# Two filter sums moved into the first product, and a wider first tile behind the switch to normed tokens, in a 16-product forward pass

## The chip, the cores and the metric

One NeuronCore of one Trainium2 chip runs the whole program in one launch. The metric is the device time of that launch in microseconds (us); a lower one is better. Matrices are float32; the weights and tokens of the large products are split into a high and a low part (type fp32r), and each 128x128 weight block is used in three matmuls: high by high, high by low, low by high.

## The reference, cut to what matters

Two blocks of a transformer run one after the other on 256 tokens of width 1024. What the change touches is the Conformer convolution at the very start and the gated feed-forward products of the second block.

```python
def conformer_conv(h, w_pw1, b_pw1, w_dw, b_dw, ln_g, ln_b, w_pw2, b_pw2):
    u = h @ w_pw1 + b_pw1                      # "pw1": 16 tiles of 128 channels
    a, gate = jnp.split(u, 2, axis=-1)
    u = a * jax.nn.sigmoid(gate)
    u = causal_depthwise_conv(u, w_dw) + b_dw  # width 31: the filter sums
    u = jax.nn.silu(layernorm(u, ln_g, ln_b))
    return u @ w_pw2 + b_pw2                   # "pw2": 8 tiles

def _swiglu(h, wg, wu, wd):                    # "gu2", "gu3": gate and up, 44 tiles
    return (jax.nn.silu(h @ wg) * (h @ wu)) @ wd
...
h = _rms_norm(x, norm_ffn[l]) * (1.0 + sc2) + sh2
x = x + g2 * _swiglu(h, ffn_gate[l], ffn_up[l], ffn_down[l])
```

## The kernel before

Sixteen products run in a fixed order on TensorE (PE): pw1, pw2, gu0, dn0, mixd, outd, gu1, dn1, mixe, oute, gu2, dn2, mixo, outo, gu3, dn3. Channels lie on partitions, the 256 tokens on the free axis. A product has tiles of 128 output channels; a tile takes `kts` blocks (8 in most products), a block is three matmuls, so a tile of 8 blocks has 24 matmuls. All PE matmuls of the products have one line, L558. The first tiles of a product (its `lead`, 4 in pw1 and 3 in gu2) run interleaved block by block; the others run one after the other. PSUM banks go round: five in pw1, six in gu2 and gu3.

Weights come in units of eight blocks (512 KB). The SP queue loads unit v into one of five `raw` buffers once VectorE (DVE) has made the low part of unit v-5. ScalarE (ACT) makes the high part (`whi`), DVE the low part (`wlo`), both about five units ahead of PE. Each engine has its own instruction queue, worked in order, and the order is written out by hand in four programs that loop over the same tiles.

The convolution stage. In pw1 the even tiles are gates and the odd ones values. DVE takes each tile from its bank (`tmp<-ps`), ACT applies the sigmoid on even tiles, and DVE writes the gated tile `U[n]` after each odd one. The causal filter needs shifted copies of U, and gets them through memory: `taps_out(j)` writes U of channel tile j to the tensor `uscr` (one DMA of 143.5 KB on ACT's queue, for tile 7 on SP's), and `taps_in(j)` reads it back shifted into `UR[j % 3]` with four DMAs of 142 KB. For j = 0, 1, 2 ACT issues these reads, at the pw1 tiles that `READ_BACK` names (9, 11, 13); for j = 3 to 7 SP issues them, after it has waited for the last U and written it to `uscr`. On PE, `taps(j)` (line L598) is the filter sum of channel tile j: 64 matmuls of 32 columns of diagonal filter blocks `DG[j % 3]` by `UR[j % 3]`, into bank 5 or 6. It waits for `DG`, for all four reads of `UR` and, from j = 2, for the copy of an earlier sum out of its bank. All eight filter sums stand behind pw1. At pw1 tile 7 SP also writes an attention table to memory (`scratch<-bvec`, 432 KB from 12 partitions).

```python
READ_BACK = (9, 11, 13)
...
product("pw1", ..., after, ...)      # calls after(nt) when tile nt is issued
for j in range(KD):
    taps(j)
```

The feed-forward stages of the second block. gu2 and gu3 (f = 2, 3) start before the norm of their tokens is known: tiles 0 to 5 use raw tokens and 258 columns, 256 tokens and two that carry a shift. Meanwhile ACT and DVE prepare normed tokens in the other pair of buffers (`HH`, `HL`), the low part in `normed_low(kt)`, which signals `nhl`; from tile 6 on (`NORMED`) PE uses these and 256 columns, waiting for `nhl` block by block. `broad(nt, kt)` says which blocks of a feed-forward product move 258 columns although 256 would do: in gu0 and gu1 all of tile 3 (`BROAD_TILE`), in dn0 to dn3 the first four blocks of the leading tiles, in gu2 and gu3 none behind tile 5. In the products of `BROAD_AFTER`, pw1 among them, the first three blocks after other matmuls are also made wide (`fresh`). The two extra columns lie behind the tokens at T:T+2; DVE fills them once at the start and signals `edge`.

Of the kernel before, what the change touches and what calls it, by code (L numbers as in the profile page):

```python
# [14 lines left out]
T = 256  # L15
D = 1024
KD = 8
# [37 lines left out]
SHIFT = 4  # L55
GATHERED = 6
RINGED = 3
READ_BACK = (9, 11, 13)


class Product:
# [156 lines left out]
NORMED = {2: 6, 3: 6}  # L218
NORMED_PUT = {2: "oute", 3: "outo"}
# [177 lines left out]
def program(nc, wall, ada, x_in, vec_in, crow_in, wq_in, row_in, rel_in, k128, kdist, koh, kmask, kbias, scratch, uscr, out):  # L397
    with ExitStack() as ctx:
        S = Signals(lambda name: ctx.enter_context(nc.semaphore("s_" + name)))
# [13 lines left out]
        HH = [sb(f"HH{i}", [P, KD, TW], F32R) for i in range(2)]  # L413
        HL = [sb(f"HL{i}", [P, KD, TW], F32R) for i in range(2)]
        RST = [sb(f"RST{i}", [P, T]) for i in range(2)]
        SQA, SQB = sb("SQA", [P, T]), sb("SQB", [P, T])
        ident, ones, bones = sb("ident", [P, P]), sb("ones", [P, P]), sb("bones", [P, P])
# [71 lines left out]
        def end_mm(name):  # L489
            return PROD[name].tile_mm[slot_of(name, PROD[name].tiles - 1 - (PROD[name].tiles - 2 in PROD[name].double))]  # L490
# [25 lines left out]
        def tensor_program():  # L516
            pe = Queue(nc.tensor)
# [70 lines left out]
            def convolution():  # L588
                def taps(j):

                    bk = bank[5 + j % 2]
                    pe.wait_ge(S.dg, j + 1)
                    pe.wait_ge(S.ur[j % 3], 64 * (j // 3 + 1))
                    if j >= 2:
                        pe.wait_ge(S.cva if j - 2 < SHIFT else S.lnx, j - 1)
                    for m in range(8):
                        for r in range(4):
                            ins = pe.e.matmul(bk[32 * r:32 * r + 32, 0:T], DG[j % 3][:, 8 * r + m, :],  # L598
                                              UR[j % 3][:, r, 4 * m:4 * m + T], start=(m == 0), stop=(m == 7))
                    pe.then_inc(ins, S.cvt)  # L600

                def over_channels(bk, t, j):

                    return pe.e.matmul(bk[:, 0:T], ones[:, :], t, start=(j == SHIFT - 1), stop=(j == KD - 1))

                def after(nt):
                    if nt == 4:
                        pe.wait_ge(S.koh, 16)
                        pe.wait_ge(S.rel, 16)
                        pe.wait_ge(S.sd, 1)  # L610
                        pe.then_inc(pe.e.matmul(bank[7][0:12, 0:NB], rels[:, :], ohs[:, :], start=True, stop=True), S.relm)

                product("pw1", HH[NORM_SET[0]], HL[NORM_SET[0]], T, norm_ready(0), after,
                        lambda kt: total(0) if kt == KD - 1 else None)
                for j in range(KD):
                    taps(j)
                    if j == SHIFT:
                        pe.wait_ge(S.bv, 1)
                        pe.wait_ge(S.lnp, SHIFT - 1)
                        pe.then_inc(pe.e.matmul(bank[7][:, 0:T], ones[:, :], SQA[:, :], start=True, stop=True), S.lnt)  # L620

                pe.wait_ge(S.cva, SHIFT + 1)
                pe.wait_ge(S.lnp, SHIFT - 1 + 2 * (GATHERED - 1))
                over_channels(bank[7], SQA[:, :], SHIFT - 1)
                pe.wait_ge(S.ev, PROD["pw1"].first_slot + PROD["pw1"].slots)
                over_channels(bank[0], SQ8[:, 0, :], SHIFT - 1)
                for j in range(GATHERED, KD):
                    pe.wait_ge(S.lnx, j + 1)
                    shift = over_channels(bank[7], CV[:, j, :], j)
                    if j == KD - 1:  # L630
                        pe.then_inc(shift, S.lnt)
                    pe.wait_ge(S.lnq, j + 1)
                    square = over_channels(bank[0], SQ8[:, j, :], j)
                pe.then_inc(square, S.lnt)
                busy(bank[5], 17)
                product("pw2", HH[LN_SET], HL[LN_SET], T, lambda kt: pe.wait_ge(S.lnl, kt + 1))

            def feed_forward(f):
                i = FFN_NORM[f]

                def after(nt):
                    if nt == 0 and f not in NORMED:
                        total(i)

                def before(kt):
                    if kt == TOTAL_AT and f in NORMED:
                        total(i)

                other = 1 - NORM_SET[i]
                later = (NORMED[f], HH[other], HL[other], T, lambda kt: pe.wait_ge(S.nhl, normed_tiles(f, kt))) if f in NORMED else None  # L650
                def broad(nt, kt):
                    return f < 2 and nt == BROAD_TILE

                def gated(kt):
                    return pe.wait_ge(S.gl, KF * f + min(kt + (2 if kt < BROAD_KTS else 1), KF))

                product(f"gu{f}", HH[NORM_SET[i]], HL[NORM_SET[i]], T + 2 if f >= 2 else T, norm_ready(i), after, before, None, later, broad)
                product(f"dn{f}", GH, GL, T, gated,
                        broad=lambda nt, kt: nt < PROD["dn0"].lead and kt < BROAD_KTS)
# [638 lines left out]
        def vector_program():  # L1298
# [187 lines left out]
            def feed_forward(f, scale):  # L1486
# [7 lines left out]
                def normed_low(kt):  # L1494
# [2 lines left out]
                    stt(HL[other][:, kt, 0:T], TX[kt % 4][:, :], mod(f - 2, 3, kt), HH[other][:, kt, 0:T].bitcast(F32),  # L1497
                        ALU.add, ALU.subtract, S.nhl)

                for s in range(2 * KF + 3):  # L1500
                    if s == 0 and f in NORMED:
                        lows(first_unit(name) + LOOK - 1)
                        inverse(NORM_RST[i])
                        normed_scaled(0)
                        normed_scaled(1)
                    if s < 2 * KF:
                        lows(low_to(name, s))
                    if s == 0 and f not in NORMED:
                        inverse(NORM_RST[i])
                    if f in NORMED and 1 <= s <= KD // 2:  # L1510
                        for kt in (2 * s, 2 * s + 1):
                            if kt < KD:
                                normed_scaled(kt)
                        normed_low(2 * s - 2)
                        normed_low(2 * s - 1)
                    if s % 2 == 0 and s >= 4:
                        m = s // 2 - 2
                        N = KF * f + m
                        dv.wait_ge(S.gh, N + 1)
                        tt(GL[:, m, :], TG[N % 3][:, :], GH[:, m, :].bitcast(F32), ALU.subtract, S.gl)  # L1520
                    if s % 2 == 0 and 2 <= s <= 2 * KF and not normed(f, s - 2):
                        N = KF * f + s // 2 - 1
                        g, u = TG[N % 3], TU[N % 2]
                        dv.wait_ge(S.silu, N + 1)
                        dv.wait_ge(S.ev, slot_of(name, s - 1) + 1)
                        if f >= 2:
                            stt(g[:, :], u[:, :], bcol[2 + N % 2][:, 0:1], g[:, :], ALU.add, ALU.mult, S.gm)
                        else:
                            tt(g[:, :], u[:, :], g[:, :], ALU.mult, S.gm)
                    if s < 2 * KF and normed(f, s):  # L1530
                        if s % 2:

                            N = KF * f + s // 2
                            g, ps = TG[N % 3], ended(name, s)
                            dv.wait_ge(S.silu, N + 1)
                            dv.then_inc(dv.e.tensor_tensor(g[:, :], ps[:, 0:T], g[:, :], ALU.mult), S.ev, 2)  # L1536
                    elif s < 2 * KF:
                        N = KF * f + s // 2
                        ps = ended(name, s)
                        if s % 2 == 0:  # L1540
                            t, b = TG[N % 3], bcol[N % 2]
                            dv.wait_ge(S.gl, max(N - 2, 0))
                            if f >= 2:
                                dv.wait_ge(S.silu, N - 1)
                        else:
                            t, b = TU[N % 2], bcol[2 + N % 2]
                            if N:
                                dv.wait_ge(S.gm, plain_pairs(f, s // 2 - 2) if s >= 4 else plain_pairs(f - 1, KF - 1) if f else 0)
                        if f >= 2:
                            dv.e.tensor_tensor(t[:, :], ps[:, 0:T], rooted(name)[:, :], ALU.mult)  # L1550
                            dv.then_inc(dv.e.tensor_copy(b[:, :], ps[:, T:T + 1]), S.ev)
                        else:
                            tt(t[:, :], ps[:, 0:T], rooted(name)[:, :], ALU.mult, S.ev)
# [625 lines left out]
```

## Time and profile before

| | us |
|---|---|
| median of three runs | 1199.04 (1198.98 to 1201.17) |
| the profiled execution, its own time | 1208.44 |
| its span | 1207.1 |
| PE busy | 1155.9 (96%) |
| VectorE busy | 883.2 (73%) |
| ScalarE busy | 655.7 (54%) |
| GpSimd busy | 84.7 (7%) |
| DMA, mean over the span | 214 GB/s |

The profiled execution took 9.4 us longer than the median of the runs. PE's busy time counts a matmul from its start to its modelled end, and matmuls overlap, so that share says only that PE has nearly always one in hand; how fast they follow each other must be read from counts in a stretch or from start times.

### The profile page before, as it was taken

How to read it: one execution, taken by the hardware profiler on the slowest of the kernel's cores; microseconds unless marked ns; L12 is line 12 of the kernel's file. 1: busy time of each engine (PE TensorE's matmuls, PEld its weight loads, DVE VectorE, ACT ScalarE, POOL GpSimd, SP SyncE). 2: the span in 40 equal slices, each digit the busy share in tenths (PEclk: the TensorE clock that was granted, in tenths of full speed). 3: DMA queues.
4: the chain of work that ended last, by engine and by line, in shares of the span. 5: the costliest groups of instructions: out<-in, count | busy, mean ns of one | idle time of the engine just before them, and what ended most of it. 6: DMA issues, size and time to landing. Idle time of an engine off the chain costs nothing.

```text
span 1207.1 us, 24464 instructions
## 1 busy us (share of the span) xinstructions
PE 1155.9 (96%) x9868; PEld 1108.5 (92%) x9868; DVE 883.2 (73%) x1645; ACT 655.7 (54%) x1153; POOL 84.7 (7%) x95
## 2 busy tenths in 40 slices
PE   7889999999998999999998889999999889999999
PEld 7859999999987999999988779999999768999999
DVE  6737698878665798887888668888886666855542
ACT  6427665445445654546555777544455776644431
POOL 2021000001000100002100011000010222000000
PEclk9999999999989999999998999999999999999999
DMA  7862698889742488887743324899987433566562
GB/s 271 252 179 105 222 323 289 265 275 316 239 158 88 140 298 287 278 292 268 273 130 111 105 88 158 269 327 321 325 277 231 142 117 122 195 192 190 176 192 71
DMA packets 81412, 258.28 MB, mean 214 GB/s; under 512 B 9032, under 2 KB 22036, under 8 KB 81300
## 3 DMA queue, kind: packets, MB, share of 16 engines
q1 hardware_dynamic: 78564, 253.94, 63.6%
q10 hardware_dynamic: 2736, 2.77, 0.8%
q8 instruction: 79, 1.29, 0.4%
q14 instruction: 33, 0.27, 0.1%
HBM read 254.01 MB, written 2.67 MB: 213 GB/s over the span
## 4 chain that ended last, share of the span: by engine, by line
PE 82%; DVE 7%; ACT 3%; issue 3%; DMA 2%; POOL 1%; ACTq 0%; DVEq 0%; POOLq 0%
PE ps L558 75%; PE ps L598 2%; DMA UR<-uscr 1%; DVE wlo L1303 1%; PE ps L663 1%; PE ps L671 1%; PE ps L662 1%; DMA raw<-wall 1%; PE ps L667 1%; ACT oS L889 1%; ACT tmp L889 1%; ACT whi L889 1%; PE ps L739 0%; ACT eS L889 0%; DVE RST L1346 0%
## 5 line engine op out<-in xcount | busy, mean ns | idle before, releaser
L558 PE MATMUL ps<-HH,whi 128*128 128x256 f32 (+1 forms) x2152 | 613.5, 285 | 12.2 <-DVE wlo L1303 7.7
L558 PE MATMUL ps<-HL,whi 128*128 128x256 f32 (+1 forms) x2152 | 603.9, 281 | 0.0
L558 PE MATMUL ps<-HH,wlo 128*128 128x256 f32 (+1 forms) x2152 | 603.9, 281 | 0.0
L889 ACT ACTIVATE whi<-raw 128x1024 fp32r<-128x1024 f32 (+1 forms) x364 | 381.0, 1053 | 313.3 <-PE ps L558 293.4
L1303 DVE TENSOR_TENSOR wlo<-raw,whi 128x1024 fp32r<-128x1024 f32 (+1 forms) x364 | 442.9, 1224 | 45.2 <-ACT whi L889 45.0
L558 PEld LDWEIGHTS ps<-HH,whi 128*128 128x128 f32 x2152 | 408.5, 190 | 23.6 <-issue 17.5
L558 PEld LDWEIGHTS ps<-HL,whi 128*128 128x128 f32 x2152 | 410.0, 191 | 0.4
L558 PEld LDWEIGHTS ps<-HH,wlo 128*128 128x128 f32 x2152 | 410.0, 191 | 0.0
L558 PE MATMUL ps<-GH,whi 128*128 128x256 f32 (+1 forms) x704 | 195.0, 277 | 1.7 <-DVE tmp L1536 1.3
L558 PE MATMUL ps<-GL,whi 128*128 128x256 f32 (+1 forms) x704 | 194.7, 277 | 0.0
L558 PE MATMUL ps<-GH,wlo 128*128 128x256 f32 (+1 forms) x704 | 194.7, 277 | 0.0
L558 PEld LDWEIGHTS ps<-GH,whi 128*128 128x128 f32 x704 | 132.3, 188 | 2.4 <-issue 1.7
L558 PEld LDWEIGHTS ps<-GL,whi 128*128 128x128 f32 x704 | 132.3, 188 | 0.0
L558 PEld LDWEIGHTS ps<-GH,wlo 128*128 128x128 f32 x704 | 132.3, 188 | 0.0
L1317 DVE CUSTOM_DVE_ANT_0 araw<-araw,cond 128x1024 f32<-128x1024 f32 x96 | 120.7, 1257 | 5.1 <-DMA araw<-ada 5.1
L1853 POOL TENSOR_TENSOR SQA<-SQA,ts 128x256 f32<-128x256 f32 x48 | 40.4, 842 | 684.8 <-ACT ts L889 684.2
L1536 DVE TENSOR_TENSOR tmp<-ps,tmp 128x256 f32<-128x256 f32 x38 | 16.1, 424 | 62.7 <-PE ps L558 60.8
L1303 DVE TENSOR_TENSOR tmp<-ps,RST 128x256 f32<-128x256 f32 x104 | 43.5, 420 | 21.4 <-PE ps L558 20.8
L889 ACT ACTIVATE GH<-tmp 128x256 fp32r<-128x256 f32 x88 | 35.6, 405 | 33.1 <-DVE tmp L1303 21.7
L1303 DVE TENSOR_TENSOR GL<-tmp,GH 128x256 fp32r<-128x256 f32 x88 | 36.9, 419 | 1.3 <-ACT GH L889 1.3
L1309 DVE SCALAR_TENSOR_TENSOR X<-ps,MOD,X 128x256 f32<-128x256 f32 x32 | 15.2, 479 | 30.4 <-PE ps L558 30.4
L598 PE MATMUL ps<-UR,DG 128*32 128x256 f32 x512 | 30.1, 396 | 7.3 <-DMA UR<-uscr 6.1
(223 smaller groups left out, 926.9 us busy)
## 6 DMA issues: line engine op xcount, KB each, us to landing
raw<-wall SPq DMA_DIRECT2D x363, 512.0 KB, 4.4
araw<-ada SPq DMA_DIRECT2D x96, 512.0 KB, 4.9
oBB<-kbias SPq DMA_DIRECT2D x16, 192.0 KB, 2.5
UR<-uscr SPq DMA_DIRECT2D x20, 142.0 KB, 3.0
UR<-uscr ACTq DMA_DIRECT2D x12, 142.0 KB, 12.0
aTB<-scratch SPq DMA_DIRECT2D x12, 128.0 KB
out<-X SPq DMA_DIRECT2D x8, 128.0 KB, 3.0
uscr<-U ACTq DMA_DIRECT2D x7, 143.5 KB, 10.1
```

What stands on the lines that cost most here:

```text
L558: ins = pe.e.matmul(o, l, r, start=(kt == p.order[0] and i == 0), stop=(kt == p.order[-1] and i == 2))
L598: ins = pe.e.matmul(bk[32 * r:32 * r + 32, 0:T], DG[j % 3][:, 8 * r + m, :], UR[j % 3][:, r, 4 * m:4 * m + T], start=(m == 0), stop=(m == 7))
L662: pe.e.matmul(bk[:, 0:128], q[:, 0:128], k[:, 0:128], start=True, stop=True)
L663: return pe.e.matmul(bk[:, 128:384], q[:, 128:256], k[:, 0:256], start=True, stop=True)
L667: ins = pe.e.transpose(bk[:, i * P:(i + 1) * P], s[:, i * P:(i + 1) * P], ident[:, :])
L671: pe.e.matmul(o, v(0), pt[:, 0:256], start=True, stop=False)
L889: ac.then_inc(ac.e.activation(o, i, func, **kw), sem)
L1303: dv.then_inc(dv.e.tensor_tensor(o, a, b, op), sem)
L1309: dv.then_inc(dv.e.scalar_tensor_tensor(out=o, in0=a, scalar=s, in1=b, op0=op, op1=op2), sem)
L1317: dv.then_inc(dv.e.tensor_tensor_reduce(a[:, :], a[:, :], cond[:, :], 1.0, 0.0, ALU.mult, ALU.add, MOD[:, v:v + 1]), S.ada)
L1536: dv.then_inc(dv.e.tensor_tensor(g[:, :], ps[:, 0:T], g[:, :], ALU.mult), S.ev, 2)
L1853: po.then_inc(po.e.tensor_tensor(o, a, b, op), sem)
```

## The change

The filter sums of channel tiles 0 and 1 are issued from within pw1, after its tiles 9 and 12; the loop behind pw1 starts at 2. ACT issues the reads of `UR` for channel tiles 0, 1 and 2 at pw1 tiles 5, 8 and 11. In gu2 and gu3 the eight blocks of tile 6, the first on normed tokens, move 258 columns. For that DVE writes the two columns behind the tokens of `HL[0]` and `HH[0]` anew at the start of gu2, and signals `edge` a second time, for which PE waits at tile 6.

```diff
-READ_BACK = (9, 11, 13)
+READ_BACK = (5, 8, 11)
+AMID = (9, 12)
...
                 def after(nt):
+                    if nt in AMID:
+                        taps(AMID.index(nt))
                     if nt == 4:
...
-                for j in range(KD):
+                for j in range(len(AMID), KD):
                     taps(j)
...
                 def broad(nt, kt):
+                    if f in NORMED and nt == NORMED[f]:
+                        pe.wait_ge(S.edge, 2)
+                        return True
                     return f < 2 and nt == BROAD_TILE
...
+                if f == 2:
+                    both = ident[:, 0:2 * KD].rearrange("p (k t) -> p k t", t=2)
+                    dv.wait_ge(S.xf, KD)
+                    dv.wait_ge(S.mm, end_mm(NORMED_PUT[f]))
+                    for t in (HL[0], HH[0]):
+                        ins = dv.e.tensor_copy(t[:, :, T:T + 2], both)
+                    dv.then_inc(ins, S.edge)
                 for s in range(2 * KF + 3):
```

## Rows read from the trace of the kernel before

**Rows 1.** The page's chain of work that ended last, shares of the span.
```profile
PE ps L558 75%; PE ps L598 2%; DMA UR<-uscr 1%; DVE wlo L1303 1%; PE ps L663 1%; PE ps L671 1%; PE ps L662 1%; DMA raw<-wall 1%; PE ps L667 1%; ACT oS L889 1%; ACT tmp L889 1%; ACT whi L889 1%; PE ps L739 0%; ACT eS L889 0%; DVE RST L1346 0%
```
**Rows 2.** L558 in stretches of gu1, gu2, gu3, outd; busy (matmuls), clock, DMA share.
```profile
425.00:515.00 90.00, 90.00 (x796) 90.00 (x795) 1.00 0.87 291
760.00:850.00 90.00, 90.00 (x766) 90.00 (x766) 1.00 0.91 315
1045.00:1135.00 90.00, 90.00 (x767) 90.00 (x766) 1.00 0.62 197
400.00:407.00 7.00, 7.00 (x62) 7.00 (x61) 1.00 0.45 154
```
**Rows 3.** PE's order of time at gu2's tiles 3 and 6, gu1's 3, outd's 2.
```profile
744.22 0.28 PE L558 MATMUL ps<-HH,whi 128*128 128x258 f32 x1
...
752.91 0.28 PE L558 MATMUL ps<-HH,whi 128*128 128x256 f32 x1
...
420.12 0.28 PE L558 MATMUL ps<-HH,wlo 128*128 128x258 f32 x1
...
396.24 0.28 PE L558 MATMUL ps<-HH,wlo 128*128 128x258 f32 x1
```
**Rows 4.** PE's order of time in gu3's tile 6, its last two blocks.
```profile
1038.00 0.38 PE L558 MATMUL ps<-HH,whi 128*128 128x256 f32 x1
...
1038.46 0.33 PE L558 MATMUL ps<-HH,whi 128*128 128x256 f32 x1
```
**Rows 5.** DVE's order of time around the normed tokens of gu3, gu2, and at the start.
```profile
1037.47 0.87 DVE L1309 SCALAR_TENSOR_TENSOR HL<-tmp,MOD,HH 128x256 fp32r<-128x256 f32 x2
...
740.57 1.75 DVE L1346 RECIPROCAL RST<-RST 128x256 f32<-128x256 f32 x1 [1.25 <-ACT RST L889]
...
17.20 0.79 DVE L1420 CAST HL<-ident 128x16 fp32r<-128x16 f32 x2
```
**Rows 6.** PE's order of time in pw1 (tiles 10, 13 begin) and at the first filter sum.
```profile
39.26 0.28 PE L558 MATMUL ps<-HH,whi 128*128 128x256 f32 x1
...
47.42 0.28 PE L558 MATMUL ps<-HH,whi 128*128 128x256 f32 x1
...
59.89 0.42 PE L598 MATMUL ps<-UR,DG 128*32 128x256 f32 x4 [4.15 <-DMA UR<-uscr]
```
**Rows 7.** ACT's order of time: weights, taps_out(3), first taps_in, copies of filter sums 2, 3.
```profile
33.23 2.00 ACT L889 ACTIVATE whi<-raw 128x1024 fp32r<-128x1024 f32 x2
...
39.98 0.33 ACTq L892 DMA_DIRECT2D uscr<-U  x1
...
41.54 3.09 ACTq L892 DMA_DIRECT2D UR<-uscr  x1
...
75.82 0.47 ACT L889 ACTIVATE CV<-ps,vec 128x256 f32<-128x256 f32 x1 [4.45 <-PE ps L598]
79.27 0.47 ACT L889 ACTIVATE CV<-ps,vec 128x256 f32<-128x256 f32 x1 [2.98 <-PE ps L598]
```
**Rows 8.** SP's scratch and last uscr, DVE's taking of pw1 tile 15.
```profile
37.95 0.90 SPq L1922 DMA_DIRECT2D scratch<-bvec  x1
...
62.72 0.33 SPq L1922 DMA_DIRECT2D uscr<-U  x1
...
61.68 0.42 DVE L1303 TENSOR_TENSOR tmp<-ps,RST 128x256 f32<-128x256 f32 x1
```
**Rows 9.** ACT's DMA queue (packets, MB, share), 41.5 to 47, 47 to 60; landing, 75 to 78.
```profile
q10 hardware_dynamic: 87, 0.09, 4.6%
...
q10 hardware_dynamic: 1036, 1.06, 29.5%
...
UR<-uscr SPq DMA_DIRECT2D x4, 142.0 KB, 2.9
```
**Rows 10.** All engines in two stretches of the first filter sum, clock last but two.
```profile
58.00:62.00 4.00, 2.11 (x24) 1.43 (x28) 1.46 (x2) 2.30 (x3) 0.00 (x0) 0.78 1.03 348
62.00:66.00 4.00, 3.24 (x44) 1.87 (x36) 1.29 (x3) 0.68 (x2) 0.00 (x0) 0.79 1.08 279
```

## The prediction

> **What bounds the kernel now.** I began with the page's chain of waits [rows 1]: PE's product matmuls carry 75% of it, and the filter sums (L598) and the reads behind them come next, at 2% and 1%. So two questions matter: how fast do product matmuls follow each other, and how long does PE stand in the convolution stage.
>
> For the first I counted L558 in stretches of one product each [rows 2]. In gu1, 90 us hold 796 matmuls, one in 113.1 ns. In gu2 and gu3 the same 90 us hold 766 and 767, one in 117.5 ns, although these move 256 columns too and no wait lies between them. So 256 columns have two paces. outd's last tiles show the slow one too (62 in 7 us). Tiles that move 258 columns have a third: from the start of gu2's tile 3 to that of tile 6 are 72 matmuls in 8.69 us, 120.7 ns each [rows 3]. What sets the pace? At gu1's last wide matmul, 420.12, PE goes over to 256 columns and the fast pace follows. Of the 20 places where the trace goes from wide to narrow, 18 lead to 113 ns at once; the two in outd, one of them at 396.24 [rows 3], to the slow pace, which then stays. gu2 and gu3 also enter tile 6 fast. Then blocks 6 and 7 wait for the normed tokens: the matmuls at 1038.00 and 1038.46 last 0.38 and 0.33 us where 0.28 is usual [rows 4], and DVE's low parts of these blocks were written just then, 1037.47 to 1038.34 [rows 5]. Behind these two small waits the pace is slow, up to the end of the product. I read: a small wait amid narrow matmuls can drop PE into the slow pace, a run of wide ones nearly always frees it.
>
> For the second I followed PE, ACT, SP and the DMA queues from 33 to 80 us. pw1 goes at 2.72 us a tile ((47.42 - 39.26) / 3) and ends at 59.89 - 4.15 = 55.74 [rows 6]. PE then waits 4.15 us for the reads of the first filter sum. They were issued from 41.54 on, the first issue alone taking 3.09 us [rows 7], and landed at about 59.9. Why so late: SP's scratch write went out at 37.95 [rows 8], and from 41.5 to 47 ACT's queue got 4.6% of the DMA engines' time, for 87 packets; from 47 to 60 ACT's queue moved 1036 packets [rows 9], and one channel tile's reads are 512. Once freed, a filter sum takes 3.45 us (79.27 - 75.82) [rows 7].
>
> **The change part by part.** *The wide first tile.* Tile 6 costs 24 x 120.7 ns = 2.90 us. Before, it took about 24 x 113.1 = 2.71 plus waits of 0.10 and 0.05 [rows 4] and the slow end of the tile, 2.9 as well: no difference. The wide tile reaches blocks 6 and 7 later by 18 x 7.6 ns = 0.14 us, so most of the small waits goes away, and what is left (I reckon some 0.03 us at block 7) falls among wide matmuls. Then 37 tiles, 888 matmuls, go at 113.1 in place of 117.5 ns: 3.9 us in gu2 and 3.9 in gu3, 7.8 together. Bounds: 0 for a product that stays slow, 3.9 for one that goes fast. The cover holds: DVE is busy 73% of the span, and DMA, at 0.91 [rows 2], would need 0.91 x 117.5 / 113.1 = 0.95; gu1 runs fast at 0.87, so a loss of up to 1 us in gu2 is possible and I take none. DVE's two copies at the start of gu2 are of the kind that took 0.79 us for two at most [rows 5]. They stand ahead of three low parts that PE needs only units later, and ahead of the reciprocal, before which DVE idles 1.25 us [rows 5]. So they cost nothing; without that cover, 0.2 to 0.8 us of later normed tokens.
>
> PE's wait for the copies is met long before tile 6. The Trainium skill ("TensorE: Matmul & The Clock Gate", Back-to-back issue gap) has a matmul cost its columns over 2.4 GHz plus 2.5 ns, that is 109 ns for 256 columns and 110 for 258. By it two columns more can't make what follows faster; the trace disagrees, as 113.1 and 117.5 ns stand for the same 256 columns. By the rule this part would cost 0.04 us and gain nothing.
>
> *The filter sums amid pw1.* First UR[0]. ACT reaches tile 5 after the two weight copies from 33.23, of which the first belongs to it, so the four reads go out from 34.2 to 36.0. That is ahead of the scratch write. The uncrowded latency is 2.9 us [rows 9], but weights and the write of U[2] share the queues; I take a landing at 41 (bounds 39 and, if the last reads get stuck behind the scratch write, 47.5). pw1's tile 9 ends at 39.26, where tile 10 now begins [rows 6], so PE waits 1.7 us, sums 3.45 us, and ends tiles 10 to 12 at 41 + 3.45 + 3 x 2.72 = 52.6.
>
> Then it needs UR[1]. ACT can issue these reads only behind the write of U[3] at 39.98 [rows 7], so from 40.35: that is the slot that UR[0] had, 1.2 us sooner, right behind the scratch write and among the same weight loads. The wait is thus not taken away, it is handed to the next channel tile. What would let UR[1] land sooner than UR[0] did at 59.9? Its reads may skip the 3.09 us stall of the issue; but before, all of UR[0] was issued by 47, and from then on its packets only took turns with SP's, so an earlier issue helps little. What would let it land later? UR[0]'s own 512 packets now stand ahead of the scratch write: at the mean rate of ACT's queue behind it, 1036 packets in 13 us [rows 9], and with the idle share of the queues before 38, I reckon 0.4 us net. I take 60.3. Bounds: 45, the uncrowded latency from 42.2 on, and 64.
>
> PE so waits 60.3 - 52.6 = 7.7 us. A wait of 4.15 us was followed by a clock of 0.78 and 0.79 over 8 us [rows 10]: half speed, 1.2 GHz, for 0.22 x 4 + 0.21 x 4 = 1.7 us of loss. I take the same 1.7 (up to 3.4 for the longer wait). pw1 ends at 60.3 + 3.45 + 1.7 + 3 x 2.72 = 73.6, where it was 55.74.
>
> Next is UR[3], which SP reads only after the last U. From DVE's taking of tile 15 to SP's write of U[7] it took 62.72 - 61.68 = 1.04 us [rows 8]; with 0.16 for the last matmul's end ahead of it and 0.35 for the write's issue, the first read goes out at 75.2, the last some 1.7 later, and 2.9 us on it has landed [rows 9]: 79.8. DG[3], queued on DVE behind the last U, is done sooner, and filter sum 2 (73.6 to 77.1) is hidden. Filter sum 3 starts at 79.8; before, it started at 79.27 - 3.7 = 75.6 [rows 7]. From there on, UR[4] to UR[7] (reads that follow each other on a queue that is then nearly empty), the sums, the layer norm and pw2 keep their old distances. So this part costs 79.8 - 75.6 = 4.2 us, plus 0.1 for the two times three blocks that go wide after the sums: 4.3.
>
> Queued behind ACT's earlier reads are its weight copies and sigmoids: UR[0]'s issue (1.8 us) delays one weight copy that DVE wants only at 37.8, UR[1]'s delays the sigmoid of tile 8 to about 44, and U[4] with it; PE, late itself, needs that bank five tiles on. SP's queue keeps its order. The weights of pw1 are five units ahead, so a unit that lands 1 to 2 us later stops nobody.
>
> The Trainium skill ("DMA: Bandwidth & Descriptors", Issuing engines are not separate DMA queues) says that transfers started by different engines run on the same 16 DMA engines and interleave. The trace agrees: ACT's queue moves 87 packets in 5.5 us while SP's holds the scratch write [rows 9]. This speaks against the change, since reads issued sooner still share.
>
> **The sum.** -7.8 + 4.3 = -3.5 us. The profiled execution, span 1207.1 and own time 1208.44, becomes 1203.6 and 1204.9. It lies 9.4 us above the median of the runs; I keep that distance: 1199.0 - 3.5 = 1195.5 us.
>
> **The rivals.**
>
> UR[1] lands in time. For it: its issue is 1.2 us earlier and may miss the stall; the scratch write comes from 12 partitions and may not hold every DMA engine. Against it: PE's wait before ended with the slowest share, and 47 to 60 was crowded throughout. Then pw1 ends at 52.6 + 3.45 + 3 x 2.72 = 64.2, UR[3] lands at 64.2 + 6.2 = 70.4, and the part gains 5.2 us (7.2 if UR[0] is in time too): 1199.0 - 7.8 - 5.2 = 1186.0, or 1184.0. The point from which part one changes sign is a landing of UR[1] at 60.3 - 4.3 = 56.0.
>
> The slow pace stays (slower). A place in gu2 and gu3, the end of tile 6: the rest of a small wait at block 7 leaves only three wide matmuls behind it, and outd went over to narrow ones slowly after nine. Price: the 7.8 us don't come, and the stage costs its 4.3: 1203.3. It decides for slower as soon as both products keep 117.5 ns and UR[1] lands after 58.5. For it: two in 20 switches. Against it: 18 in 20, and both products end tiles 3, 4 and 5 in the same rhythm, from which tile 6 was entered fast. If only one of them stays slow, the sum is -3.9 + 4.3, 1199.4, no change. By the Trainium skill's rule above, this rival is the rule: wide matmuls give nothing.
>
> UR[1] is later still, at 63 to 64, or the clock takes 3.4 us in place of 1.7: another 3 us, 1198.5, about no change. For it: UR[0]'s packets ahead of the scratch write, a wait nearly twice as long. Against it: DMA before 38 has room, and part of UR[0] fits in.
>
> **How the numbers follow.** About 0.2%, 2.4 us, is what a measurement here can tell from no change. Forecast, 0.48: 1195.5, its own range 1193.5 to 1197.5, of which I hold the part above 1196.6 for 0.08. UR[1] in time, 0.20. One product stays slow, 0.12. Both, 0.08. UR[1] or the clock later still, 0.12. By these, faster is 0.48 - 0.08 + 0.20 = 0.60, no change 0.08 + 0.12 + 0.12 = 0.32, slower 0.08. But cases can meet: one product at 117.5 ns with a late UR[1] gives 1199.4 + 3 = 1202.4, slower. For that I move 0.02 and 0.08 over: 0.58, 0.24, 0.18. The range takes in half of the rival below and of those above: 1185.5 to 1200.5.
>
> **What would show it.** In gu2 and gu3, 796 matmuls in 90 us, where 766 stood. In pw1, a filter sum from 41 to 44.5, a wait of PE at the second one of 7 to 8 us put down to UR, a clock below 1 there, the product's end near 73.6, and the copy of filter sum 3 near 83.5 where it was 79.27. The prediction is wrong if PE finds UR[1] landed (then 1186), if the first sum waits behind the scratch write, or if tile 7 of gu2 or gu3 goes at 117.5 ns.

## The result, and the profile after

The changed kernel takes 1209.0 us (median of 7 runs, 1204.71 to 1215.21), the one before 1199.04 (7 runs, 1196.89 to 1201.17). The ratio is 1.0063, with a 95% interval of 1.0041 to 1.0086: some 7.5 us slower, where 3.5 us faster was forecast. (The two medians lie 10.0 us apart, 0.83%, inside that interval; I go by the ratio.) The profiled execution of the changed kernel spans 1207.7 us; the profiled one of before spans 1207.1. In the traces the two look equal, in the timed runs they are not. That gap is the first thing to explain.

The page's chain that ended last, shares of the span, answers to [rows 1]:
```profile
PE ps L559 73%; PE ps L599 2%; DVE wlo L1309 1%; DMA UR<-uscr 1%; PE ps L669 1%; PE ps L668 1%; PE ps L677 1%; PE ps L673 1%; ACT whi L895 1%; ACT oS L895 1%; ACT tmp L895 1%; ACTq L898 1%; DVE X L1315 0%; ACT HH L895 0%; ACT eS L895 0%
```
A new link is in it, ACTq L898: ACT's issuing of the reads of UR now stands on the path.

The product matmuls (L559 after the change) in 90 us of gu2 and of gu3, as in [rows 2]; the columns are those shown there:
```profile
770.00:860.00 90.00, 90.00 (x796) 90.00 (x795) 1.00 0.94 331
1050.00:1140.00 90.00, 90.00 (x796) 90.00 (x796) 1.00 0.66 205
```
Here are the 796 matmuls that the prediction named, and gu2 and gu3 take 123.2 and 123.1 us from their start to dn2's and dn3's, where they took 127.1 and 127.1. So 7.85 us are gained between these two traces.

DVE's order of time at gu2's start, with the two copies (L1511) and the reciprocal of [rows 5]:
```profile
746.38 0.17 DVE L1511 CAST HL<-ident 128x16 fp32r<-128x16 f32 x1
746.46 0.17 DVE L1511 CAST HH<-ident 128x16 fp32r<-128x16 f32 x1
...
748.86 1.75 DVE L1352 RECIPROCAL RST<-RST 128x256 f32<-128x256 f32 x1 [1.11 <-ACT RST L895]
```
The copies take 0.17 us each, and DVE still idles 1.11 us ahead of the reciprocal: they cost nothing.

PE's order of time in pw1 and the convolution, the filter sums alone. First the kernel before (L598), of which [rows 6] shows only the start:
```profile
59.89 5.35 PE L598 MATMUL ps<-UR,DG 128*32 128x256 f32 x64 [4.15 <-DMA UR<-uscr]
67.18 3.66 PE L598 MATMUL ps<-UR,DG 128*32 128x256 f32 x64 [1.94 <-DMA UR<-uscr]
72.10 10.57 PE L598 MATMUL ps<-UR,DG 128*32 128x256 f32 x192 [1.26 <-issue]
```
Then the changed kernel (L599):
```profile
42.77 3.66 PE L599 MATMUL ps<-UR,DG 128*32 128x256 f32 x64 [2.65 <-DMA UR<-uscr]
...
58.88 6.59 PE L599 MATMUL ps<-UR,DG 128*32 128x256 f32 x64 [4.01 <-DMA UR<-uscr]
...
73.84 3.66 PE L599 MATMUL ps<-UR,DG 128*32 128x256 f32 x64
81.71 4.65 PE L599 MATMUL ps<-UR,DG 128*32 128x256 f32 x49 [4.21 <-issue]
```
The chain that ended last, around filter sum 1 (start, length, what):
```profile
41.05 4.28 ACTq L898
...
47.76 10.98 DMA UR<-uscr
58.74 0.14 issue
58.88 6.59 PE ps L599 x64
```
Before, PE waited 4.15 us for UR[0], 1.94 for UR[1] and 1.26 for UR[2], 7.4 us in all; now it waits 2.65 us for UR[0], 4.01 for UR[1], and 4.21 ahead of filter sum 3, 10.9 in all. The last is put down to "issue"; DMA issues tell what it was. SP's order of time, the write of U[7] and the reads of UR[3] and later ones:
```profile
75.05 0.33 SPq L1935 DMA_DIRECT2D uscr<-U  x1
...
75.48 13.36 SPq L1935 DMA_DIRECT2D UR<-uscr  x16
```
The four reads of UR[3] are issued from 75.48 to 76.87, and the last of them lands at 81.6, just ahead of the sum.

All engines in the stretches of filter sum 1 and filter sum 3; the last but two is the granted clock, as in [rows 10]:
```profile
58.00:65.00 7.00, 6.12 (x60) 3.30 (x64) 0.00 (x0) 0.22 (x1) 0.00 (x0) 0.51 0.96 281
81.00:86.00 5.00, 4.29 (x49) 2.83 (x53) 0.00 (x0) 0.00 (x0) 0.00 (x0) 0.66 0.80 171
```
Behind each of the two longer waits PE runs at its lower level, 1.2 GHz. The clock of 0.51 over 7 us is worth 3.4 us, but 0.9 us of that stretch passed while PE still stood waiting: sum 1 took 6.59 us where 3.66 is usual, 2.9 lost. At the second it is 0.34 x 5 = 1.7 us. pw2 starts at 108.7 us, where it started at 100.9. So this stage costs 7.8 us in these two traces, and eats what gu2 and gu3 gained. The terms: 3.5 us more of waits, 2.9 us more of half clock (4.6 against the 1.7 of before), 0.4 us because tiles 10 and 13 take 2.90 us with their wide blocks where 2.72 is usual, and 0.7 us because pw1's tile 9 begins at 37.23 in the one trace and at 36.54 in the other, before any sum was moved; in the second trace of the kernel before it begins at 37.11. That makes 7.5 of the 7.8 us, and the last 0.7 isn't shown to be the change's.

### The profile page after: what moved, and what is told of

Its sections match the earlier page's. It is cut to its first block, busy times and chain, and to the rows that moved or that the text cites. A ratio compares the mean times of both kernels' runs of the same rounds, so it can differ in the third digit from the quotient of the medians.

```text
span 1207.7 us, 24466 instructions
## 1 busy us (share of the span) xinstructions
PE 1151.0 (95%) x9868; PEld 1100.7 (91%) x9868; DVE 883.1 (73%) x1647; ACT 655.7 (54%) x1153; POOL 84.2 (7%) x95
## 4 chain that ended last, share of the span: by engine, by line
PE 81%; DVE 8%; ACT 4%; issue 3%; DMA 1%; POOL 1%; ACTq 1%; DVEq 0%; POOLq 0%
PE ps L559 73%; PE ps L599 2%; DVE wlo L1309 1%; DMA UR<-uscr 1%; PE ps L669 1%; PE ps L668 1%; PE ps L677 1%; PE ps L673 1%; ACT whi L895 1%; ACT oS L895 1%; ACT tmp L895 1%; ACTq L898 1%; DVE X L1315 0%; ACT HH L895 0%; ACT eS L895 0%
## 5 line engine op out<-in xcount | busy, mean ns | idle before, releaser
L559 PE MATMUL ps<-HH,whi 128*128 128x256 f32 (+1 forms) x2152 | 611.2, 284 | 12.5 <-DVE wlo L1309 8.0
L559 PE MATMUL ps<-HL,whi 128*128 128x256 f32 (+1 forms) x2152 | 601.6, 280 | 0.0
L559 PE MATMUL ps<-HH,wlo 128*128 128x256 f32 (+1 forms) x2152 | 601.3, 279 | 0.0
L559 PEld LDWEIGHTS ps<-HH,whi 128*128 128x128 f32 x2152 | 408.7, 190 | 24.5 <-issue 18.5
L559 PEld LDWEIGHTS ps<-HL,whi 128*128 128x128 f32 x2152 | 408.7, 190 | 0.4
L559 PEld LDWEIGHTS ps<-HH,wlo 128*128 128x128 f32 x2152 | 408.5, 190 | 0.0
L559 PE MATMUL ps<-GH,whi 128*128 128x256 f32 (+1 forms) x704 | 195.3, 277 | 1.7 <-DVE tmp L1549 1.3
L559 PE MATMUL ps<-GL,whi 128*128 128x256 f32 (+1 forms) x704 | 195.0, 277 | 0.0
L559 PE MATMUL ps<-GH,wlo 128*128 128x256 f32 (+1 forms) x704 | 194.9, 277 | 0.0
L559 PEld LDWEIGHTS ps<-GH,whi 128*128 128x128 f32 x704 | 132.3, 188 | 2.4 <-issue 1.7
L559 PEld LDWEIGHTS ps<-GL,whi 128*128 128x128 f32 x704 | 132.4, 188 | 0.0
L559 PEld LDWEIGHTS ps<-GH,wlo 128*128 128x128 f32 x704 | 132.3, 188 | 0.0
L599 PE MATMUL ps<-UR,DG 128*32 128x256 f32 x512 | 33.3, 423 | 10.9 <-DMA UR<-uscr 6.7
L599 PEld LDWEIGHTS ps<-UR,DG 128*32 128x32 f32 x512 | 19.6, 121 | 23.4 <-issue 16.1
```

The costliest lines, as they stand in the source:

```text
L559: ins = pe.e.matmul(o, l, r, start=(kt == p.order[0] and i == 0), stop=(kt == p.order[-1] and i == 2))
```

## The experiments

Two questions were open. On the pace, theory A (the prediction's) says that small waits drop PE into the slow pace and wide matmuls free it; theory B, that the pace comes and goes from one execution to the next of the same program, so that the slow gu2 and gu3 of the first trace were a chance of that execution. On the convolution, theory 1 says that UR[1] is held up by what stands beside it in the queues, SP's scratch write above all, and that sums amid pw1 delay its end and so the last U. Each kernel below was timed against the kernel before on the same chip; three sets of runs were made, and before had medians of 1201.4, 1201.45 and 1203.57 us in them.

**The wide tile alone.** The diff's part in `broad` and the two copies on DVE; the order of sums and reads as before.
```
+                    if f in NORMED and nt == NORMED[f]:
+                        pe.wait_ge(S.edge, 2)
+                        return True
```


> The wide first tile of gu2 and gu3 alone, with DVE's two copies; the filter sums stay behind pw1. Theory A (the slow pace of gu2 and gu3, 117.5 ns a matmul, is in every execution of the kernel before): 7.8 us faster, ratio 0.9935. Theory B (it was in the profiled execution of the kernel before, which took 9.4 us longer than its timed ones, and those go at 113 ns without help): the same time, ratio 0.999 to 1.001; its profile shows 113 ns in both.

Measured: 1202.37 us (12 runs), ratio 1.0009 (0.9985 to 1.0032). In its trace gu2 and gu3 take 123.2 us each. No gain of this part is seen in the timed runs; the interval leaves room for 1.8 us at most, not for 7.8.

**The sums amid pw1 and the earlier reads alone.**
```
-READ_BACK = (9, 11, 13)
+READ_BACK = (5, 8, 11)
+AMID = (9, 12)
```


> The two filter sums amid pw1 and the earlier reads alone. The profile of the change has pw2 start 7.8 us later (108.72 against 100.88), so both theories expect about 7.8 us more at the start of pw2. Theory A: the total is 7.8 us slower, 1.0065. Theory B: the total is as slow as the whole change, 7 to 10 us, 1.006 to 1.008, as the wide tile gives nothing to timed executions; should its profile fall on slow gu products, they are counted at 117.5 ns.

Measured: 1208.33 us (12 runs), ratio 1.0057 (1.0031 to 1.0083). The whole loss comes from this part. In its trace pw2 starts at 104.1: PE waits 2.88 us for UR[0], 1.95 for UR[1] and 3.22 ahead of sum 3, and sums 3 and 4 take 9.96 us where 7.11 is usual. gu2 and gu3 both go slowly in it. It is of the slowest of the kernel's 12 runs (1214.44), 6.1 us above their median.

**The kernel before, as it is.**

> The kernel before, unchanged, for a second profile of it. Theory A: 766 matmuls in 90 us in gu2 and gu3 again, and an own time of the profiled execution near the timed ones. Theory B: the pace of gu2 and gu3 differs from the first profile, and the profiled time is shorter by 3.9 us for each product that goes fast. Ratio 1.000 in both.

Measured: 1202.42 us, ratio 1.0016 (0.9993 to 1.0039). The trace spans 1199.2 us, 7.9 less than the first one of the same program. Product matmuls (L558) in gu2 and gu3:
```profile
760.00:850.00 90.00, 90.00 (x797) 90.00 (x796) 1.00 0.94 329
1043.00:1133.00 90.00, 90.00 (x797) 90.00 (x796) 1.00 0.65 203
```
The kernel without the wide tile has the fast pace in both. Its two small waits in tile 6 are there (the matmul at that place follows after 223 ns in gu2, where 113 is usual). So the waits don't decide. Nor does a run of wide matmuls: pw2 opens with three wide blocks, and behind them (L558) it is fast in the first trace of the kernel before,
```profile
104.00:116.00 12.00, 12.00 (x108) 12.00 (x107) 1.00 0.57 200
```
and slow in this second one of the same program:
```profile
107.00:119.00 12.00, 12.00 (x104) 12.00 (x103) 1.00 0.63 224
```
Theory A falls here.

**The scratch write moved.** SP writes the attention's table only after the convolution's reads.
```
-                if nt == 7:
-                    sp.wait_ge(S.bv, 1)
-                    load(scratch, bvec[:, :].unsqueeze(1).broadcast_to([12, NR, NB]), S.bd)
+                pass
...
+            sp.wait_ge(S.bv, 1)
+            load(scratch, bvec[:, :].unsqueeze(1).broadcast_to([12, NR, NB]), S.bd)
             for nt in tiles("pw2"):
```


> The kernel before with SP's write of the attention table moved from pw1's tile 7 to ahead of pw2; nothing else. My reading of the profiles is that this write, from 12 partitions, holds 12 of the 16 DMA engines from 41 to 46.5 us and so delays UR[0] and what is queued behind. Then UR[0] lands about 4 us sooner, near 55, so at pw1's end, and PE's wait of 4.15 us goes: 4 to 5 us faster, unless UR[1] or UR[2] is then late (2 us). Rival (the queues are full with weights and reads anyway): less than 1.5 us.

Measured: 1199.09 us, ratio 0.9986 (0.9966 to 1.0006). PE's filter sums (L598) in its trace:
```profile
55.94 3.66 PE L598 MATMUL ps<-UR,DG 128*32 128x256 f32 x64
62.34 5.35 PE L598 MATMUL ps<-UR,DG 128*32 128x256 f32 x64 [2.74 <-DMA UR<-uscr]
68.60 10.57 PE L598 MATMUL ps<-UR,DG 128*32 128x256 f32 x192 [0.91 <-issue]
```
UR[0], issued from 41.8 on, lands at 52.2, where before it took from 41.5 to 59.8. The wait of 4.15 us ahead of the first sum [rows 6] is gone, the one for UR[1] is 2.74 us for 1.94, the one for UR[2] 0.91 for 1.26: 3.7 us less in all. pw2 starts at 97.4, 3.5 us sooner; the timed gain is 1.7 us at the middle, and not told from none; the 4 to 5 us of the expectation it isn't.

**The sums amid pw1, with the write moved.** The two edits above together.
```
+READ_BACK = (5, 8, 11)
+AMID = (9, 12)
```

> The two filter sums amid pw1 and the earlier reads (no wide tile), with SP's write of the attention table moved ahead of pw2. Theory 1 (UR[1] lands late because its reads stand behind that write): UR[1] lands near 50 to 51, before tile 12 ends at 54.4, PE waits only for UR[0] (3.4 us), pw1 ends at 66, filter sum 3 starts at 72.3 against 75.5 before: 3 us faster than before, 0.997, level with the kernel that only moves the write. Theory 2 (weights and reads fill the queues without it): UR[1] lands after 56 and the kernel is as slow as before or slower.

Measured: 1203.56 us, ratio 1.0031 (1.0011 to 1.0051). PE's filter sums in its trace:
```profile
42.36 3.66 PE L599 MATMUL ps<-UR,DG 128*32 128x256 f32 x64 [2.37 <-DMA UR<-uscr]
...
54.38 3.66 PE L599 MATMUL ps<-UR,DG 128*32 128x256 f32 x64
...
66.42 3.66 PE L599 MATMUL ps<-UR,DG 128*32 128x256 f32 x64
73.75 7.11 PE L599 MATMUL ps<-UR,DG 128*32 128x256 f32 x128 [3.66 <-issue]
```
UR[1] has landed at 52.4 and PE doesn't wait for it, as theory 1 says. The expectation's 3 us of gain (0.997) did not come. But 2.37 and 3.66 us of waits stay, and the timed runs are still slower than before. Removing the UR[1] wait isn't enough for a gain. This trace is of the fastest of the kernel's 12 runs (1198.99), 4.6 us under its median, so it doesn't show the typical one.

**The sums later.** The scratch write is in its old place.
```
+READ_BACK = (5, 8, 11)
+AMID = (12, 15)
```

> As the filter sums amid pw1 alone, but after its tiles 12 and 15 (AMID = (12, 15)) in place of 9 and 12; reads at tiles 5, 8, 11, the attention table's write where it was, no wide tile. If the loss of the change is PE standing inside pw1 in front of reads that have not landed, which delays the last U and so UR[3]: UR[0] is there at 47.4, tile 15 ends near 59, its U is written near 60.5, UR[1] has landed (57 to 59), UR[3] lands near 67 and filter sum 3 starts at 67 to 70, 5 to 8 us sooner than before: 0.993 to 0.996. If moving sums into pw1 costs by itself (clock, pace behind the sums, ACT's issue): no faster than before.

Measured: 1201.09 us, ratio 0.9991 (0.9973 to 1.0009). PE waits neither for UR[0] nor for UR[1] in pw1 (landed at 42.1 and 57.4; the sums start at 47.5 and 59.6), and the loss is gone. But the gain that the expectation took for this case (0.993 to 0.996) did not come either: UR[2] lands at 67.5, PE waits 4.37 us ahead of sum 2, and sums 2 to 4 take 13.01 us where 10.57 is usual. pw2 starts at 98.8.

**Two sums later, the write moved, UR[3] read sooner.** `READ_BACK = (5, 8, 11)`, `AMID = (11, 14)`, and SP reads UR[3] and UR[4] ahead of its wait for the last U:
```
             for j in range(RINGED, KD):
+                if j == RINGED + len(AMID):
+                    sp.wait_ge(S.u, KD)
+                    sp.wait_ge(S.uz, 2)
+                    load(uscr[KD - 1], U[:, KD - 1, :], S.uw[KD - 1])
```


> Filter sums 0 and 1 after pw1's tiles 11 and 14, reads at tiles 5, 8, 11, the attention table's write moved ahead of pw2, and SP reads UR[3] and UR[4] before it waits for the last U; no wide tile. No wait of PE in pw1: it ends at 55.7 + 2 x 3.45 + 0.1 = 62.7, filter sum 3 starts at 66.2 and pw2 at 66.2 + 25.3 = 91.5 against 100.8: 9 us faster, 0.992. If UR[2], read at tile 11, lands only near 65: 2 us less.

Measured: 1194.24 us (6 runs), ratio 0.9943 (0.9923 to 0.9963): faster than before. pw2 starts at 97.2. The forecast for it (0.992, pw2 at 91.5) was too good: UR[3] lands only at 70.1, the sum waits 2.38 us for it and the next two run at half clock for part of their time (8.80 us where 7.11 is usual).

**The wide tile on the kernel with the write moved alone, and on the last one.** The edit is that of the first experiment.

> The attention table's write moved ahead of pw2, and the wide first tile of gu2 and gu3; the filter sums behind pw1. To be held against the same kernel without the wide tile (1199.1 us, within 4.4 us over 12 executions). Theory A (timed executions without the wide tile often go at 117.5 ns in gu2 or gu3): 2 to 8 us faster than that one. Theory B (they rarely do): the same within 0.1%, about 0.9985 of the kernel before, 113 ns in its profile.

Measured: 1199.44 us, ratio 0.9978 (0.9958 to 0.9998), against 0.9986 without that tile. Both products are fast in its trace, and pw2 starts at 98.6.

> The kernel of early reads (two sums behind tiles 11 and 14 of pw1, the reads back sooner, the table of the attention written last, UR[3] read before the last of U) with the wide first tile for the normed tokens added in gu2 and gu3. It took 1194.2 (ratio 0.994) without that tile. Theory B (the slow pace of gu2 and gu3 is rare in timed executions, so the wide tile is worth nothing): 1194 to 1196, ratio 0.993 to 0.997. Rival A (the slow pace is frequent, the wide tile gives back up to 7.8 us): 1187 to 1190, ratio 0.988 to 0.991. In its profile gu2 and gu3 run at 113.3 ns a matmul under both; pw2 starts at 97 us.

Measured: 1196.74 us (9 runs), ratio 0.9943 (0.9921 to 0.9965), against 0.9943 without it. In none of the three comparisons does the wide tile show a gain; each leaves some 2 to 4 us open, not 7.8. pw2 starts at 94.4 in this trace (97 was expected). Product matmuls in gu2 and gu3 of this last trace:
```profile
754.00:844.00 90.00, 90.00 (x796) 90.00 (x796) 1.00 0.93 329
1035.00:1125.00 90.00, 90.00 (x767) 90.00 (x766) 1.00 0.64 197
```
gu3 has the slow pace although its tile 6 is wide, and no small wait is left in it. The expectation's "under both" was wrong: it took from theory A that a wide run frees the pace.

**Two more profiles of unchanged programs.**

> The kernel before, unchanged, profiled once more. Theory B (the pace of 113.3 or 117.8 ns behind a small wait differs from one execution to the next of one program): gu2 and gu3 have the same two small waits at tile 6, and each goes at one or the other pace; span near 1199 when both are at 113.3, near 1207 when both are at 117.8. Rival A (the waits set the pace): 117.8 ns in both, 127 us each.

> The changed kernel, profiled once more. Both theories have gu2 and gu3 at 113.3 ns (123.2 us each). Theory 1 on the sums: UR[1] lands 2 to 5 us after tile 12 ends, the engine waits for it, then waits 3 to 5 us more for UR[3]; pw2 starts between 104 and 109 us against 100.6 to 100.9 before. Rival: the conversion of the first profile was one bad execution, and pw2 starts at 100 or sooner.

The profiled executions took 1211.18 us (before) and 1206.86 (after), one of each. The kernel before (L558), gu2 and gu3:
```profile
766.00:856.00 90.00, 90.00 (x796) 90.00 (x795) 1.00 0.93 329
1048.00:1138.00 90.00, 90.00 (x766) 90.00 (x765) 1.00 0.63 196
```
The changed kernel (L559), the same:
```profile
762.00:852.00 90.00, 90.00 (x797) 90.00 (x796) 1.00 0.93 330
1045.00:1135.00 90.00, 90.00 (x766) 90.00 (x765) 1.00 0.63 195
```
Both have one product fast and one slow, with the same small waits in both products of before and none in both of after. The span of this third trace of before is 1209.9 us, 10.7 longer than the second one's, and only 3.9 of that is gu3's pace: its granted clock is 0.983 over the whole span, against 0.991 in the second trace and 0.990 in the first. The expectation that the changed kernel has two fast ones was wrong as well. Its filter sums in this second trace:
```profile
42.23 5.35 PE L599 MATMUL ps<-UR,DG 128*32 128x256 f32 x64 [2.81 <-DMA UR<-uscr]
56.59 3.66 PE L599 MATMUL ps<-UR,DG 128*32 128x256 f32 x64 [0.58 <-DMA UR<-uscr]
68.62 3.66 PE L599 MATMUL ps<-UR,DG 128*32 128x256 f32 x64
75.47 7.11 PE L599 MATMUL ps<-UR,DG 128*32 128x256 f32 x128 [3.19 <-issue]
```
Here UR[1] costs 0.58 us in place of 4.01, and pw2 starts at 100.8. So the 7.8 us of the first trace are one execution's, too. The rival that the expectation named, pw2 at 100 or sooner, all but came.

**The earlier reads without any sum amid pw1.** The kernel of ratio 0.9943 with one line changed; all eight sums follow pw1, the scratch write comes last. With `AMID` empty, SP's place for the last U (`RINGED + len(AMID)`) is again ahead of UR[3], so this kernel differs from the one with the scratch write moved alone by `READ_BACK = (5, 8, 11)` and nothing else, and from the one with sums at 9 and 12 and the write moved by the place of these two sums alone (the loop in SP's program is written otherwise, its order is the same).
```
-AMID = (11, 14)
+AMID = ()
```

> The same kernel of early reads with no sum amid pw1: all eight filter sums after it, UR[0] to UR[2] read back behind vector-work tiles 5, 8 and 11, the attention's table written last; UR[3] can be read only once sum 0 has freed its buffer, after pw1. Theory 1 (UR[0] to UR[2] wait in their buffers, pw1 runs through and ends near 59 us, then three sums of 3.5 to 4 us run on, and the wait goes to UR[3], which is issued at about 63 and lands 8 to 10 us later): sums 0 to 2 end at 70, UR[3] lands at 72, pw2 starts at 94 to 97, ratio 0.993 to 0.998. Rival 2 (the sums amid pw1 carry the gain, since they free the buffer of UR[3] ten us sooner): pw2 starts at 99 to 101, ratio 0.998 to 1.001. It also shows the rate at which the path through the memory lands once sums are not amid the product.

Measured: 1193.46 us (6 runs), ratio 0.9918 (0.9897 to 0.9938), the fastest of all and better than either theory had it (pw2 at 94 at the soonest, 0.993). PE's filter sums:
```profile
55.91 17.62 PE L599 MATMUL ps<-UR,DG 128*32 128x256 f32 x320
74.09 10.57 PE L599 MATMUL ps<-UR,DG 128*32 128x256 f32 x192
```
and the chain that ended last in this stretch (start, length, what):
```profile
29.91 26.07 PE ps L559 x230
55.98 17.55 PE ps L599 x320
73.53 0.63 PE ps L623 x2
74.16 10.50 PE ps L599 x192
84.66 2.37 PE ps L605 x10
```
PE waits for nothing from 29.91 to 84.66; pw2 starts at 91.7. pw1 ends at 55.9, SP writes the last U at 57.06, issues UR[3] at 59.63, once sum 0 has freed its buffer, and it lands at 66.3, when sum 2 ends (66.5). The reads of UR[1] tell why the earlier ones are in time. DMA issues with their median from issue to landing, in this kernel (40.5 to 43 us)
```profile
UR<-uscr ACTq DMA_DIRECT2D x4, 142.0 KB, 6.2
```
and in the changed kernel (41 to 49 us), where the scratch write went out at 38.65:
```profile
UR<-uscr ACTq DMA_DIRECT2D x4, 142.0 KB, 9.7
```
ACT's four issues take 2.13 us together here, and 7.13 there. The write isn't all that moves the landing, though. UR[1], whose first read is issued at 40.3 to 41.1 in all eight traces with the earlier reads, lands at 56.5, 56.7, 57.4 and 58.7 with the write in its old place, and at 50.9, 52.4, 55.3 and 56.4 with it moved; the last two are the kernels with sums at 11 and 14.

What the traces of these three kernels show, in us (pw2's start; lengths of gu2 and gu3):

| kernel | pw2 starts | gu2 | gu3 |
|---|---|---|---|
| before, three traces | 100.9, 100.6, 101.5 | 127.1, 123.1, 123.1 | 127.1, 123.2, 127.1 |
| after, two traces | 108.7, 100.8 | 123.2, 123.1 | 123.1, 127.1 |
| sums and reads alone | 104.1 | 127.1 | 127.0 |

## Why the prediction was wrong

*The wide tile: the step that failed.* "Then 37 tiles, 888 matmuls, go at 113.1 in place of 117.5 ns: 3.9 us in gu2 and 3.9 in gu3, 7.8 together" holds between the two first traces within 0.1 us, and no gain shows in the timed runs: 1.0009, 0.9978 against 0.9986, 0.9943 against 0.9943. The reading behind it, "a small wait amid narrow matmuls can drop PE into the slow pace, a run of wide ones nearly always frees it", is not the cause in either half. The two small waits stand in gu2 and gu3 of all nine traces without the tile, and of those 18 products 12 are fast and 6 slow; in the five traces with the tile 2 of 10 are slow, both with no small wait left and straight behind the wide tile. These counts are too small to say that the shares differ. The pace comes with the execution; agreement of the first two traces was luck. And "I keep that distance" was the error of method: the prediction itself noted that its trace lay 9.4 us above the timed runs, and of these 9.4 it was about to remove 7.8. An execution that far above the median has something that the median doesn't, and the slow pace in two products was a candidate. It isn't the only one: the third execution of before took 1211.18 us with one slow product and a lower mean clock. And timed executions have slow products too: the trace of the fastest kernel, with gu2 slow, took 1192.94 us, under its median of 1193.46. With 0 in place of -7.8, its own sum is 1199.0 + 4.3 = 1203.3, the time of its rival "the slow pace stays", to which it gave 0.08. What was measured beyond that is the size of the other part, below.

*The rule on the pace.* The Trainium skill ("TensorE: Matmul & The Clock Gate", Back-to-back issue gap) gives the figure that the prediction took, columns over 2.4 GHz plus 2.5 ns, for an isolated matmul, and says that in a stream of weight loads and matmuls both together set the spacing; so it was not the rule for this stream. The traces show two spacings for the same 256 columns at a granted clock of 1.00, 113.3 and 117.8 ns, and neither is the 109 that the prediction worked out. That the wide tile gains nothing is what the prediction read from that rule; the runs bear out the result and not the reason.

*The sums amid pw1: direction right, size too small.* By its steps, against the first trace: UR[0] landed at 42.6 (forecast 41, bounds 39 and 47.5), so PE waited 2.65 us for 1.7. UR[1] landed at 58.7 (60.3). Tiles 10 to 12 ended later than forecast, so the wait was 4.0 us for 7.7. The half clock took 2.9 us for 1.7, within the bound of 3.4. pw1's end came at 73.9 (73.6): errors that cancelled. Then two terms were missed. The reads of UR[3] took 4.75 us from the last issue to the landing and not 2.9; U[7]'s write and UR[4]'s reads, issued right behind at 77.4, were in flight with them, which may be why; no run tests it. So sum 3 started at 81.7 and not 79.8. And PE's idle time ahead of it was followed by a second stretch of half clock, 1.7 us: sums 3 and 4 took 8.80 us and not 7.11. 6.1 + 1.7 = 7.8 us for 4.3. Over three traces of this arrangement pw2 starts at 104.5 on average, against 101.0 in three of before: +3.5 (+3.1 when the trace of the wide tile alone, with 102.8, is counted with before, whose convolution stage it has). The timed loss of this part is 0.57%, 6.9 us, with 3.7 to 10 as its interval; 4.3 lies inside, near its lower end. What makes up the rest of 6.9 isn't shown: no trace is of a typical timed execution for sure, and more frequent half clock is only the candidate.

*Where the expected cover was.* The wait for UR was handed on, as argued: from UR[0] to UR[1] and on to UR[3]. What the prediction didn't see is that the sums were the wrong half of the change: with the write moved and the reads at 5, 8 and 11, the sums at 9 and 12 alone make the difference between 1.0031 and 0.9918. A sum put ahead of tiles 10 and 13 moves pw1's end, and with it the last U and all that SP reads behind it; without them the same earlier reads make the three first sums run on behind pw1, and these 10.6 us (55.9 to 66.5) cover the trip of UR[3]. With the write moved, the ratio is 1.0031 with sums at 9 and 12, 0.9943 with sums at 11 and 14 and UR[3] read sooner, 0.9918 with none. The whole gain is 9.9 us (0.82% of 1203.57; 9.3 us of it show at pw2's start, 91.7 against 101.0). Moving the write alone gave 1.7 us of it, not told from nothing (0.9986); the earlier reads on top of that brought 0.9918. The reads alone with the scratch write in its old place were not tried, so how much of their gain hangs on the write's move isn't known.

*The DMA queues.* That an earlier issue of UR[1] "helps little" held wherever the scratch write stood beside it: it landed at 58.7 and 56.5 in the changed kernel and at 56.7 with the sums and reads alone. Without that write it landed at 52.4 and 50.9, but also at 55.3 and 56.4, so what else holds it up isn't known. For UR[0] in its old place the write's part is plainer: it landed at 59.8, 60.2, 59.9 and 61.6 with the write beside it (before, and the wide tile alone), and at 52.2 and 53.4 with the write moved. The prediction named the write as what made the wait, and then took its price from the kernel as it stood.

## What to carry to other kernels

When the profiled execution lies well above the timed median, take a second profile of the unchanged kernel, or at least don't price an edit by what may be that excess. Work that fills a wait at the end of a stage can cost more than the wait when it is put ahead of what the next wait hangs on: issue the transfers sooner and leave the order of the engine alone, then look again. Look also for the transfer that stands beside the late one and isn't needed yet.

## What the runs showed of the hardware

- TensorE with 256 columns at a granted clock of 1.00 goes at 113.3 or 117.8 ns a matmul. Which, stays in gu2 and gu3 from tile 7 to the end, and differs among executions of one program (gu3 of before: 127.1, 123.2, 127.1 us). What sets it stays open; neither small waits nor a wide tile does so by itself.
- The stretches of low clock differ among executions as well. All engines in 70 us of mixd, the last column but two being the clock, first in the third trace of the kernel before:
```profile
310.00:380.00 70.00, 67.81 (x490) 62.68 (x488) 44.62 (x139) 34.80 (x83) 0.00 (x0) 0.90 0.48 162
```
then in the second trace of the same program:
```profile
310.00:380.00 70.00, 66.52 (x507) 60.67 (x506) 47.28 (x151) 36.64 (x90) 0.00 (x0) 0.98 0.51 174
```
mixd took 78.4 us in the one and 74.1 in the other; in the kernel with the earlier reads alone, where no line of mixd was changed and its clock was 1.00, it took 72.5. Such differences can hide or feign some 4 to 6 us in a stage far from the edit.
- After a wait PE may run a filter sum at 1.2 GHz or not. In the changed kernel's first trace none followed the wait of 2.65 us (3.66 us for the sum) and one the wait of 4.01 (6.59); in its second trace one followed 2.81 us (5.35) and none 3.19 (two sums in 7.11).
- An engine's DMA issue can itself stall behind another engine's large write: ACT's first read of UR[1] took 4.28 us to issue with the scratch write ahead, and its four issues took 2.13 us together with it moved. That held in all eight traces with the earlier reads: 6.6 to 7.1 us with the write ahead, 2.1 without.
